# The launch of a long single-core transformer kernel: four edits to the order of its first loads, splits and sums

## The reference

```python
def rmsnorm(x, g):
    y = x * lax.rsqrt(jnp.mean(x * x, axis=-1, keepdims=True) + EPS)
    return y * g

def even_mixer(xn, w_in, conv_a, pool_w, pool_scale, w_out):
    z = xn @ w_in                      # 1024 x 2048
    h, gb, gc, u = jnp.split(z, [512, 1024, 1536], axis=-1)
    y = jnp.concatenate([short_conv_mixer(h, gb, gc, conv_a),
                         pool_mixer(u, pool_w, pool_scale)], axis=-1)
    return y @ w_out
...
h = h + even_mixer(rmsnorm(h, ev_norm_mix[i]), ...)
h = h + cross_attn(rmsnorm(h, xa_norm[layer]), mem, ...)
...
```

## Time and profile before

| | us |
|---|---|
| median of 3 runs | 2387.12 (2386.99 to 2393.14) |
| profiled execution, whole | 2385.82 |
| its span, first to last instruction | 2383.9 |
| TensorE busy in the span | 2336.1 |
| mean granted TensorE clock | 0.994 |

### The profile page before, as it was taken

How to read it: one execution, slowest core, us unless ns; L and a number is a source line. 1 busy time by engine, 2 the same in 40 slices (tenths; PEclk the granted TensorE clock), 3 DMA queues, 4 the chain that set the end, 5 groups by cost and what they waited for, 6 DMA issues and landing times.

```text
span 2383.9 us, 33637 instructions
## 1 busy us (share of the span) xinstructions
PE 2336.1 (98%) x14448; PEld 2089.6 (88%) x14448; DVE 1794.4 (75%) x1835; ACT 1370.1 (57%) x1348; POOL 118.7 (5%) x94
## 2 busy tenths in 40 slices
PE   7999999999999999999999999999999999999999
PEld 7989999788988888888888888888889999888999
DVE  5856557675788888888888888887677676767665
ACT  5535445364577777777777776777455344645342
POOL 3001000001100000000000000000210001301000
PEclk9999999999999999999999999999999999999999
DMA  7644455453499999999999999996333655333553
GB/s 235 221 147 154 166 200 172 150 200 119 167 364 347 353 355 354 350 351 348 351 349 356 349 351 361 340 369 210 129 107 124 212 177 176 123 107 106 180 174 107
DMA packets 309691, 566.90 MB, mean 238 GB/s; under 512 B 12386, under 2 KB 137601, under 8 KB 309408
## 3 DMA queue, kind: packets, MB, share of 16 engines
q1 hardware_dynamic: 304752, 559.34, 66.4%
q10 hardware_dynamic: 4784, 5.35, 0.7%
HBM read 563.60 MB, written 1.05 MB: 237 GB/s over the span
## 4 chain that ended last, share of the span: by engine, by line
PE 87%; DVE 7%; DMA 3%; ACT 2%; issue 0%; POOL 0%; ACTq 0%; POOLq 0%; DVEq 0%
PE bank L1019 23%; PE bank L801 15%; PE bank L1037 11%; PE bank L650 9%; PE bank L785 7%; PE bank L638 6%; PE bank L253 5%; DVE wL L205 3%; PE bank L660 2%; ACT wH L234 2%; PE bank L1370 2%; PE bank L1318 2%; PE bank L626 1%; DMA raw<-in_od_moe_gu 1%; DMA raw<-in_ev_w_in 1%; DVE arena L205 1%
## 5 line engine op out<-in xcount | busy, mean ns | idle before, releaser
L205 DVE TENSOR_TENSOR wL<-raw,wH 128x2048 fp32r<-128x2048 f32 (+2 forms) x544 | 1210.4, 2233 | 351.0 <-ACT wH L234 348.0
L234 ACT ACTIVATE wH<-raw 128x2048 fp32r<-128x2048 f32 (+2 forms) x544 | 1014.7, 1867 | 498.8 <-PE bank L801 103.9
L1019 PE MATMUL bank<-wH,ra 128*128 128x512 f32 x1792 | 577.2, 393 | 1.2 <-DVE wL L205 0.9
L1019 PEld LDWEIGHTS bank<-wH,ra 128*128 128x128 f32 x1792 | 336.5, 188 | 71.9 <-issue 1.5
L801 PE MATMUL bank<-ra,wH 128*128 128x256 f32 x2112 | 383.6, 284 | 5.4 <-DVE ra L208 5.4
L1019 PE MATMUL bank<-wL,ra 128*128 128x512 f32 x896 | 348.7, 389 | 0.0
L801 PEld LDWEIGHTS bank<-ra,wH 128*128 128x128 f32 x2112 | 329.5, 192 | 8.1 <-DVE ra L208 6.9
L801 PE MATMUL bank<-ra,wL 128*128 128x256 f32 x1056 | 298.8, 283 | 0.0
L1037 PE MATMUL bank<-wH,ra 128*128 128x512 f32 x896 | 287.6, 391 | 0.3 <-DVE ra L205 0.2
L650 PE MATMUL bank<-wH,ra 128*128 128x512 f32 (+2 forms) x800 | 223.2, 361 | 0.5 <-DVE ra L208 0.5
L801 PEld LDWEIGHTS bank<-ra,wL 128*128 128x128 f32 x1056 | 202.7, 192 | 0.0
(11 more groups left out here) (212 smaller groups left out, 2558.9 us busy)
## 6 DMA issues: line engine op xcount, KB each, us to landing
raw<-in_od_moe_gu SPq DMA_DIRECT2D x224, 1024.0 KB, 6.3
raw<-in_od_moe_down SPq DMA_DIRECT2D x112, 1024.0 KB, 6.6
raw<-in_ev_ffn_gu SPq DMA_DIRECT2D x22, 1024.0 KB, 5.1
raw<-in_ffn_w_gate SPq DMA_DIRECT2D x22, 1024.0 KB, 5.4
raw<-in_ffn_w_up SPq DMA_DIRECT2D x22, 1024.0 KB, 5.1
raw<-in_ffn_w_down SPq DMA_DIRECT2D x22, 1024.0 KB, 4.8
raw<-in_xa_wkv SPq DMA_DIRECT2D x16, 1024.0 KB, 5.3
raw<-in_od_pw_w SPq DMA_DIRECT2D x12, 1024.0 KB, 5.0
```

Of the source, the lines that this page charges most:

```text
L205: self.op.tensor_tensor(out, a, b, op).then_inc(*self.sig.up(name))
L234: self.op.activation(out, a, ACT.Copy, **kw).then_inc(*self.sig.up(name))
L1019: m = p.op.matmul(out[:, :], a, b, start=half == 0 and c == 0 and i == 0, stop=half == 1 and c == 3 and i == 2)
```

## The change

- ScalarE no longer waits for cols ahead of its four loads (the wait stays ahead of the first scaling of x).
- Block 1 is loaded in four parts as well, by SP right behind x, rounded and subtracted by quarters, and multiplied chunk by chunk; it has four semaphores of its own. pe_fm_first gets an offset nb0 for its products.
- The squares of x stand between the roundings of block 1's quarters, instead of behind the rounding of block 2.
- TensorE's product for the mean stands between the two products of z0's first block instead of behind both, so it takes bank 5 and that block's second product bank 6. ScalarE's root and VectorE's reciprocal, the scaling of z12 and the copy up stand ahead of the split of block 4 instead of behind it.
- cst is issued behind block 2 instead of block 1, inv ahead of block 4 as before, memT ahead of block 5 instead of 4.

```diff
@@ -297,7 +297,7 @@
         self.pe2, self.act2, self.dve2 = (signal(n) for n in ("pe_more", "act_more", "dve_more"))
         self.raw_in = [signal(f"raw_in{i}", 16) for i in range(NR)]
         self.more_in = [signal(f"more_in{i}", 16) for i in range(2)]
-        self.got = {n: signal(f"{n}_in", 16) for n in ("x0", "x1", "x2", "x3", "w0", "w1", "w2", "w3", "cst", "cols", "inv", "mem", "rows", "pos", "router",
+        self.got = {n: signal(f"{n}_in", 16) for n in ("x0", "x1", "x2", "x3", *(f"w{b}{j}" for b in range(2) for j in range(4)), "cst", "cols", "inv", "mem", "rows", "pos", "router",
                                                        "mem2_0", "mem2_1", "gate_b", "conv_b")}
         self.stored = signal("stored", 16)
         self.signals = [self.pe, self.act, self.dve, self.pool, self.pe2, self.act2, self.dve2, *self.raw_in,
@@ -507,6 +507,16 @@
         h, n = self.half_of[i], self.blocks[i][1]
         return self.w_hi[:, h * 2048:h * 2048 + n], self.w_lo[:, h * 2048:h * 2048 + n]
 
+    def first_part(self, v, b, j):
+
+        return v[:, 2048 * b + 512 * j:2048 * b + 512 * j + 512]
+
+    def first_load(self, engine, b, j):
+        c0 = 1536 + 256 * b
+        engine.op.dma_start(self.first_part(self.raw, b, j).rearrange("p (c n) -> p c n", c=2),
+                            self.w["ev_w_in"][0][256 * j:256 * j + 256, c0:c0 + 256].rearrange("(c p) n -> p c n", p=128)
+                            ).then_inc(*self.got[f"w{b}{j}"].up("w"))
+
     def landed(self, i):
 
         return self.raw_in[i % NR].of(("raw", i))
@@ -548,9 +558,12 @@
         for j in range(4):
             s.op.dma_start(self.hT[:, 2 * j:2 * j + 2, :], d["xT"][256 * j:256 * j + 256, :].rearrange("(c p) t -> p c t", p=128)
                            ).then_inc(*got[f"x{j}"].up("x"))
+        for j in range(4):
+            self.first_load(s, 1, j)
         for i, (parts, n, split) in enumerate(self.blocks):
-            if i == self.index["z12", 1] + 3:
+            if i == self.index["z8", 0]:
                 s.op.dma_start(self.smb[:, :], d["inv"]).then_inc(*got["inv"].up("inv"))
+            if i == self.index["z8", 1]:
                 s.op.dma_start(self.memT, d["memT"].rearrange("(c p) t -> p c t", p=128)).then_inc(*got["mem"].up("mem"))
             if i == self.index["in", 0, "mla", 0] + 2:
                 s.wait_ge(*self.dve.of("flag"))
@@ -565,9 +578,9 @@
                     s.wait_ge(*self.pe.of(("block", i - NR)))
             slot = self.raw_in[i % NR]
             place = self.raw[:, (i % NR) * 2048:(i % NR) * 2048 + 2048]
-            for view, src in parts if i else []:
+            for view, src in parts if i > 1 else []:
                 s.op.dma_start(view(place), src).then_inc(*slot.up(("raw", i)))
-            if i == 1:
+            if i == self.index["z0", 0]:
                 s.op.dma_start(self.cst[:, :], d["cst"]).then_inc(*got["cst"].up("cst"))
         outv = self.out_d.rearrange("(c p) t -> p c t", p=128)
         for c in range(0, C, 2):
@@ -608,14 +621,14 @@
 
         return x[c] if isinstance(x, list) else (x[0][:, c, :], x[1][:, c, :])
 
-    def pe_fm_first(self, p, s, tag, k, x, x_ready, freed, order=None, w_ready=None):
+    def pe_fm_first(self, p, s, tag, k, x, x_ready, freed, order=None, w_ready=None, nb0=0):
 
         order = list(order or range(k))
         if w_ready:
             wh, wl = (v.rearrange("p (c n) -> p c n", c=k) for v in self.halves(self.index[tag]))
         else:
             wh, wl = self.pe_block(p, tag, k)
-        outs = [self.bank(p, (*s, j), *freed(j))[:, 0:256] for j in range(2)]
+        outs = [self.bank(p, (*s, nb0 + j), *freed(nb0 + j))[:, 0:256] for j in range(2)]
         for c in order:
             if w_ready:
                 p.wait_ge(*w_ready(c))
@@ -625,11 +638,13 @@
                 for i, (a, b) in enumerate(passes(wh[:, c, js], wl[:, c, js], *self.chunk(x, c))):
                     m = p.op.matmul(outs[j], a, b, start=c == order[0] and i == 0, stop=c == order[-1] and i == 2)
                 if c == order[-1]:
-                    m.then_inc(*self.pe.up((*s, j), *([("block", self.index[tag])] if j else [])))
-
-    def pe_fm_block(self, p, s, tag, per, k, x, x_ready, freed, nb0):
+                    m.then_inc(*self.pe.up((*s, nb0 + j), *([("block", self.index[tag])] if j else [])))
+
+    def pe_fm_block(self, p, s, tag, per, k, x, x_ready, freed, nb0, between=None):
         wh, wl = self.pe_block(p, tag, k)
         for j in range(per):
+            if j and between:
+                between()
             nb, js = nb0 + j, slice(j * 128, (j + 1) * 128)
             out = self.bank(p, (*s, nb), *freed(nb))[:, 0:256]
             for c in range(k):
@@ -669,12 +684,11 @@
     def pe_mixer(self, p):
         x_ready = lambda c: (self.dve.of(("mix", "lo", c)))
         scaled = lambda z: (lambda nb: (self.dve, (z, "copy", nb)))
-        block = lambda z, n: self.pe_fm_block(p, (z,), (z, n), 2, 8, self.X8, x_ready, scaled(z), 2 * n)
-        self.pe_fm_first(p, ("z12",), ("z12", 0), 8, self.X8, x_ready, scaled("z12"), None,
-                         lambda c: self.dve.of(("w_lo", 0, c // 2)))
-        block("z12", 1)
-        block("z0", 0)
-        self.pe_total(p, "mix")
+        block = lambda z, n, between=None: self.pe_fm_block(p, (z,), (z, n), 2, 8, self.X8, x_ready, scaled(z), 2 * n, between)
+        for b in range(2):
+            self.pe_fm_first(p, ("z12",), ("z12", b), 8, self.X8, x_ready, scaled("z12"), None,
+                             lambda c, b=b: self.dve.of(("w_lo", b, c // 2)), 2 * b)
+        block("z0", 0, lambda: self.pe_total(p, "mix"))
         block("z0", 1)
         block("z8", 0)
         self.pe_stat(p, "mem0")
@@ -1456,26 +1470,25 @@
 
     def act_mixer(self, a):
         got = self.got
-        w_hi, _ = self.halves(0)
-        part = lambda v, j: v[:, 512 * j:512 * j + 512]
+        part = self.first_part
         for j in range(4):
-            a.op.dma_start(part(self.raw, j).rearrange("p (c n) -> p c n", c=2),
-                           self.w["ev_w_in"][0][256 * j:256 * j + 256, 1536:1792].rearrange("(c p) n -> p c n", p=128)
-                           ).then_inc(*got[f"w{j}"].up("w"))
+            self.first_load(a, 0, j)
         a.wait_ge(*got["cols"].of("cols"))
         for j in range(4):
             a.wait_ge(*got[f"x{j}"].of("x"))
             for c in (2 * j, 2 * j + 1):
                 a.cp(("mix", "hi", c), self.X8[0][:, c, :], self.hT[:, c, :], scale=self.col("ev_norm_mix", c))
-            a.wait_ge(*got[f"w{j}"].of("w"))
-            a.cp(("w_hi", 0, j), part(w_hi, j), part(self.raw, j))
-        self.act_next = 1
-        self.act_blocks(a, ("z12", 0))
+            a.wait_ge(*got[f"w0{j}"].of("w"))
+            a.cp(("w_hi", 0, j), part(self.w_hi, 0, j), part(self.raw, 0, j))
         for j in range(4):
             a.do(("mix", "sq", j), self.sq[:, 2 * j:2 * j + 2, :], self.hT[:, 2 * j:2 * j + 2, :], ACT.Square)
+            a.wait_ge(*got[f"w1{j}"].of("w"))
+            a.cp(("w_hi", 1, j), part(self.w_hi, 1, j), part(self.raw, 1, j))
+        self.act_next = 2
+        self.act_blocks(a, ("z12", 0))
         self.act_blocks(a, ("z12", 1))
+        self.act_total(a, "mix")
         self.act_blocks(a, ("z0", 0))
-        self.act_total(a, "mix")
         a.op.dma_start(self.rows[:, :], self.d["rows"].partition_broadcast(128)).then_inc(*got["rows"].up("rows"))
         a.op.dma_start(self.posi[:, :], self.d["pos"]).then_inc(*got["pos"].up("pos"))
         a.op.dma_start(self.router, self.w["od_router"][0].rearrange("(c p) e -> p c e", p=128)
@@ -2041,7 +2054,6 @@
         return ("s0", "h", 7) if l == 0 else ("ffn2", 0, "scaled", "u", F2 // 256 - 1)
 
     def scalar_program(self, a):
-        a.wait_ge(*self.got["cols"].of("cols"))
         self.act_next = 0
         self.act_mixer(a)
         self.act_cross(a, 0)
@@ -2125,25 +2137,25 @@
 
     def dve_mixer(self, v):
         v.wait_ge(*self.got["cols"].of("cols"))
-        w_hi, w_lo = self.halves(0)
-        for j in range(4):
-            for c in (2 * j, 2 * j + 1):
-                self.dve_x(v, "mix", "ev_norm_mix", 0, c, self.X8)
-            at = slice(512 * j, 512 * j + 512)
-            v.wait_ge(*self.act.of(("w_hi", 0, j)))
-            v.tt(("w_lo", 0, j), w_lo[:, at], self.raw[:, at], w_hi[:, at].bitcast(F32), ALU.subtract)
-        self.dve.mark(("w_lo", 0))
-        self.dve_next = 1
+        part = self.first_part
+        for b in range(2):
+            for j in range(4):
+                for c in (2 * j, 2 * j + 1) if b == 0 else ():
+                    self.dve_x(v, "mix", "ev_norm_mix", 0, c, self.X8)
+                v.wait_ge(*self.act.of(("w_hi", b, j)))
+                v.tt(("w_lo", b, j), part(self.w_lo, b, j), part(self.raw, b, j), part(self.w_hi, b, j).bitcast(F32), ALU.subtract)
+            self.dve.mark(("w_lo", b))
+        self.dve_next = 2
         z, up, pp = self.z, self.up_, self.pp
```

(2 more changed lines are left out.)

## The result

| | before | changed |
|---|---|---|
| median of 20 runs each, us | 2390.80 (2385.60 to 2402.16) | 2385.12 (2381.48 to 2391.91) |
| ratio, with 95% interval | | 0.9975 (0.9964 to 0.9986) |
| profiled execution's span, us | 2383.9 | 2386.9 |
| TensorE's first product, us | 11.39 | 9.09 |
| z8 block 1 done, us | 55.80 | 50.44 |

The ratio is a gain of 6.0 us, 3.3 to 8.6 by the interval; the medians alone differ by 5.7; the forecast was 6.5. Over the whole run the interval does not tell the forecast from rivals A (8.1) and B (4.7 to 5.6). I therefore follow one mark, here called **the measure**: the moment at which VectorE begins to scale the last product of z8 block 1 out of its bank, 55.80 us before.

A forecast was written before the change was run, and what follows sets the result against it. TensorE, busy 2336.1 of 2383.9 us, was the bound, its launch a matter of bytes in order. Earlier z0 block 0 (4.74) plus the bank wait (1.72) gave 6.5 us: 2387.12 to 2380.6, range 2377.0 to 2386.0.

The forecast's parts named there:

- rivals A: Launch loads: the early hole in DMA traffic goes, landings up to 1.6 us sooner; gain up to 8.1 us, chance 0.2.
- B: Launch splits pile up on ScalarE, z0 block 0 split at 23.7 beside GpSimd; gain 4.7 to 5.6 us, chance 0.2.
- The lag of 0.61 MB: Launch loads: each lands 0.61 MB of queue traffic after its last byte, as the slowest DMA engine lags.
- Step 1: ScalarE's loads without the cols wait: issued 2.3 us sooner, last quarters land at 11.9, TensorE starts at 7 to 9.
- Steps 3 and 4: z12 block 1 ends at 21.3; z0 block 0, split at 21.9, starts then instead of 26.64: gain 4.7 us.
- Step 5: Mean inside z0 block 0: no wait for GpSimd, and the bank wait of 1.72 us goes with 2.4 to spare.
- Step 6: z8 block 0 late next: lands at 28.2, split by 32.8, wanted at 34.1, so 1.3 us to spare.
- C: TensorE stays at its slow level through both z12 blocks, 0.211 us a matmul; gain only 1.5 us, chance 0.07.
- D: Attention stretches of the second part: more granted clock at 0.83, 3.4 us per 20 us stretch; slower, 2394, chance 0.04.

The follow-up runs named there:

- changed, wait back: The changed kernel with the wait for cols put back ahead of ScalarE's loads; the measure came at 52.15 us.
- before again: The kernel before, profiled once more without any edit; the measure came at 56.15 us.

## Why the prediction was right, and where it was off

**The size.** Lead at the measure: 55.80 - 50.44 = 5.4 us in the first pair of executions, 56.15 - 49.59 = 6.6 in the second, 6.0 in the mean. Forecast 6.5, measured over the whole 6.0. The second part of the forecast, that a lead at 60 us stands at the end, agrees with the mean of the runs; in the profiled pair it did not stand.

The time itself was forecast at 2380.6, with 2379.3 to 2381.6 as the forecast's own range, and came out at 2385.12, inside the wide range of 2377 to 2386 by 0.9 us. The forecast started from 2387.12, the median of three runs of before; twenty runs gave 2390.80. That accounts for 3.7 us of the 4.5, the smaller gain for 0.8. That the time still fell into the range is owed to the room left for rivals and scatter, not to the mechanism.

**Bytes.** The lag of 0.61 MB was a good estimate: at 281 and 368 GB/s, 4.98 MB had been moved when z0 block 0 landed at 16.4 and 6.68 MB when z0 block 1 landed at 21.0, 0.60 and 0.61 MB past their last bytes. The landings came 1.3 and 1.4 us sooner than in my sum because the early hole went.

**Step 1.** TensorE's start, 7 to 9, was 9.09 and 9.18. x's first part was delayed, from 3.9 to 5.5, when both queues started together. The Trainium skill (DMA: Bandwidth & Descriptors, section Issuing engines are not separate DMA queues) says that transfers begun by several engines interleave on the same DMA engines, and to that the delay agrees; but the time of the issue did more here than save time on a sequencer, since the first 12 us moved 243 to 261 GB/s with the wait and 277 to 286 without it. The delay did not bring the small gain of rival B. The first scaling ran at the same moment all the same, 6.89 against 6.94, and that is chance: before, the table load of 1.28 us stood behind ScalarE's own issues, which ended at 5.6, now behind x. With the table loaded early x is used as it lands, at 5.95. The last quarters landed by 10.4, 11.9 foreseen; ScalarE came to the last one at 11.66.

**Steps 3 and 4, the mis-sized term.** I let TensorE pause between chunks from 7 to 9 on and end block 1 at 21.3, so that the split of z0 block 0, 21.9, would be last. The split was at 21.9 in the changed kernel and 22.0 in its second execution. But TensorE had no pause and was its own bound: 9.09 + 28 x 0.212 + 68 x 0.12 = 23.2, measured 23.3. The gain at this place was 3.3 us (first pair) and 4.9 (second, 27.4 - 22.5), not 4.7. What failed is the cost of 96 matmuls: I counted the slow level at the end of block 0 as an "if", where it took 17 to 28 matmuls. That the split came at the very time that I gave it is luck: the load landed 1.3 us sooner than in my sum, and the three quarters beside GpSimd took 2.9 us more (1.36 to 1.79 against 0.69), which I had priced at nothing. For the block itself I had the row of 3.15 and chose 2.29; it took 2.82.

**Step 5.** The bank's wait went, but the sizes were off. The first bank was emptied at 30.9 and wanted at 32.4: 1.5 us to spare, 2.4 foreseen. GpSimd's sum was ready at 19.8 and wanted at 26.2, 6.5 us to spare instead of 1.9, as TensorE came later and the squares sooner. The kernel with the mean put back prices the pause at 1.29 us in the changed order. TensorE's own way from z0 block 0 to the measure, pauses left out, is 27.1 us in the changed kernel and 27.45 before, which closes the sum of the first pair: 3.3 + 1.7 + 0.35 = 5.35. Why it is shorter with the mean inside the block, no run shows.

**Step 6.** z8 block 0 was split at 34.9 (32.8 foreseen), because the root ran at 28.19 and not at 25.6: TensorE came to the mean at 26.2 and not at 24.8, and the table load waits for the mean's product (26.89 <-PE) instead of standing ahead of it. It was still in time, by some 0.5 us.

**Rival A** had its condition, the hole went and the landings came 1.3 to 1.4 us sooner, but not its gain, since the loads were not the bound. **B** was the case in one point, the splits beside GpSimd, and would have set z0 block 0 at 21.9 and not at 23.7. **C**, the slow level, is the one that cost: 0.5 to 1.4 us of the path, not 5. **D** is seen below.

## What was given back

The lead of 5.35 us in the first pair stands unchanged at 301 us, by the table loads of ScalarE (158.75 to 153.40, 300.89 to 295.54), and is 2.3 at the next (409.95 to 407.65). The stretch of 330 to 350 between them, in the first execution of the changed kernel and in its second:

```profile
330.00:350.00 20.00, 20.00 (x120) 16.58 (x119) 10.14 (x8) 7.87 (x7) 0.00 (x0) 0.83 0.41 137
```

```profile
330.00:350.00 20.00, 20.00 (x146) 17.36 (x145) 12.83 (x10) 9.14 (x7) 0.00 (x0) 1.00 0.50 168
```

The clock granted there is 0.83 in the first and 1.00 in the second; 26 matmuls fewer at 0.12 are the 3.05 us that went. Both executions of before have 1.00 there; of the other ten, three have 0.91 (one of them the kernel before with the mean moved) and seven 1.00. So rival D's condition does occur, but not in every execution of the changed kernel. The lead was 3.7 us at 640, -1.1 at 1660 and -3.0 at the end. Between ScalarE's table loads near 640 and 1660 us, the experts, the 14 executions took from 1019.1 us (before) to 1032.2 (changed, wait back), before again 1024.3, changed 1023.9 and 1027.8. In the slowest one TensorE waits 6.7 us in 13 places for splits there; before, 0.9 us in 2. Executions of one kernel differ by 5 us in this stretch alone, so no single span can show a change of 6. That the launch has a part in it I can't exclude: the ten executions of the changed kernel and its variants took 1026.3 us in the mean and the four of before and its variants 1022.5, too few of each, and the ratio of the runs speaks against it. It stays open.

## What to carry to other kernels

Follow a change at the launch by a mark just behind it, not by the span: the mark repeated to 0.35 and 0.85 us where whole runs scatter by 10 to 17. When a wait goes, look for what comes next behind it: the wait for cols alone brought z0 block 0 forward by 2.9 us but the measure by 2.5, and the mean alone removed a pause of 1.72 us and gave 1.0, since GpSimd's sum was not ready. The two alone are 3.5 of the 6.0; the rest is that of the quarters, the squares and the order of loads together. When an engine has no pause left, add up its own instructions at the rate that it really has at that time, its slow first ones included.

## What the runs showed of the hardware that I had not expected

- The slow level of TensorE at the start lasted from 3.1 to 6.2 us behind its first product in executions with the same order of work (changed 6.2 and 3.8), and cost 0.092 us more for each matmul of 256 columns. The granted clock in the rows of those stages says 1.00 all the same, also where a matmul takes 0.212 us. With useless matmuls ahead the useful ones ran at 0.12 from the first one on, also behind a pause of 2.13 us.
- ScalarE's queue joining SP's 2.3 us later costs both: 243 to 261 GB/s over the first 12 us, against 277 to 286 when the two start together, some 0.3 MB or 1 us of all later landings. Why, no run shows.
- Quarters of a subtraction interleaved with GpSimd's additions took two to two and a half times their time, but GpSimd's additions ran faster so than beside whole blocks: 5.84 us against 7.92.
